# A hybrid attention block on one Trainium2 core: all tensors behind the small constants move back by 64 bytes in their partition

## What is computed

```python
def modulate(x, g, shift, scale):
    return rms_norm(x, g) * (1.0 + scale[:, None, :]) + shift[:, None, :]

# per layer l (latent stream xl, context stream xc)
pl = jnp.split(modulate(xl, g_mix[l], sh1, sc1) @ w_in[l], IN_OFFSETS, axis=-1)
pc = jnp.split(modulate(xc, g_mix[l], csh1, csc1) @ w_in[l], IN_OFFSETS, axis=-1)
oa_l = neighbourhood_attention(qa_l, ka_l, va_l, ka_c, va_c, na_rpb[l])     # 4 heads, "NA"
ob_l = mlstm_output(hb_l, pl[6], ml_head_gain[l])                           # 4 heads, both directions, "ML"
oc_l = blocked_attention(qc_l, concat(kc_l, kc_c), concat(vc_l, vc_c), MLA_SCALE)  # 8 heads, "MLA"
mix_l = jnp.concatenate([flat_heads(oa_l), ob_l, flat_heads(oc_l)], axis=-1) @ w_out[l]
xl = xl + gt1[:, None, :] * mix_l
xl = xl + gt2[:, None, :] * swiglu(modulate(xl, g_ffn[l], sh2, sc2), w_ffn_in[l], w_ffn_out[l])
# the context stream goes through the same weights in layer 0 only
```

## Time and profile before

| what | value |
|---|---|
| median of 3 runs | 2232.1 us |
| lowest and highest run | 2230.06 and 2235.55 us |
| span of the profiled execution | 2231.9 us |
| mean granted TensorE clock in it | 0.979 |
| PE busy | 2102.4 us, 94% of the span |
| DVE, ACT, POOL busy | 53%, 34%, 29% |

### The profile page before, as it was taken

How to read it: one execution, slowest core, us unless ns; L and a number is a source line. 1 busy time by engine, 2 the same in 40 slices (tenths; PEclk the granted TensorE clock), 3 DMA queues, 4 the chain that set the end, 5 groups by cost and what they waited for, 6 DMA issues and landing times.

```text
span 2231.9 us, 30181 instructions
## 1 busy us (share of the span) xinstructions
PE 2102.4 (94%) x11834; PEld 1733.9 (78%) x11834; DVE 1185.5 (53%) x2119; ACT 751.4 (34%) x1221; POOL 644.4 (29%) x820
## 2 busy tenths in 40 slices
PE   7888999989989999999999998889998989999999
PEld 4777788866668888888888877778866657888887
DVE  7467524468875666166436566663368864212111
ACT  4333323456663211111111233423266643222222
POOL 1210301220002333333333430141221014555555
PEclk9999989999999999999999999999899999999999
DMA  7301431110002233233223210021110002322233
GB/s 289 104 19 31 145 102 67 39 47 10 10 10 67 91 127 104 76 114 132 95 95 114 95 50 20 20 68 33 43 48 19 10 10 77 102 95 95 95 95 104
DMA packets 76242, 165.58 MB, mean 74 GB/s; under 512 B 5192, under 2 KB 46664, under 8 KB 75088
## 3 DMA queue, kind: packets, MB, share of 16 engines
q1 hardware_dynamic: 75728, 163.28, 22.0%
q10 hardware_dynamic: 384, 0.47, 0.1%
HBM read 161.63 MB, written 2.10 MB: 73 GB/s over the span
## 4 chain that ended last, share of the span: by engine, by line
PE 79%; DVE 11%; issue 4%; ACT 4%; PEld 1%; POOL 1%; DMA 1%; PEldq 0%; DVEq 0%; SPq 0%; ACTq 0%; POOLq 0%
PE psum L1093 22%; PE psum L1095 21%; PE psum L1094 21%; PE psum L1691 1%; DVE naptlo L2097 1%; PE psum L1144 1%; PE psum L1721 1%; PE psum L1175 1%; PE psum L1446 1%; PE psum L1331 1%; PE psum L1460 1%; PE psum L1397 1%; DVE maplo L2348 1%; PE psum L1216 1%; PE psum L1398 1%
## 5 line engine op out<-in xcount | busy, mean ns | idle before, releaser
L535 POOL TENSOR_TENSOR wlo<-raw,whi 128x256 fp32r<-128x256 f32 x816 | 644.1, 821 | 1579.6 <-ACT whi L560 1579.6
L1093 PE MATMUL psum<-hhi,whi 128*128 128x512 f32 (+1 forms) x1640 | 588.7, 359 | 16.8 <-DVEq L1894 8.6
L1094 PE MATMUL psum<-hlo,whi 128*128 128x512 f32 (+1 forms) x1640 | 579.5, 353 | 0.0
L1095 PE MATMUL psum<-hhi,wlo 128*128 128x512 f32 (+1 forms) x1640 | 578.6, 353 | 0.0
L560 ACT ACTIVATE whi<-raw 128x1024 fp32r<-128x1024 f32 x204 | 215.7, 1059 | 888.2 <-PE psum L1095 881.4
L1093 PEld LDWEIGHTS psum<-hhi,whi 128*128 128x128 f32 x1640 | 313.4, 191 | 72.9 <-issue 18.8
L1095 PEld LDWEIGHTS psum<-hhi,wlo 128*128 128x128 f32 x1640 | 313.0, 191 | 42.5
L1094 PEld LDWEIGHTS psum<-hlo,whi 128*128 128x128 f32 x1640 | 313.3, 191 | 39.9 <-issue 0.2
L2524 DVE TENSOR_TENSOR ffuf<-ffsa,psum 128x768 f32<-128x768 f32 (+1 forms) x44 | 36.1, 821 | 331.5 <-ACT ffsa L1043 324.8
L2509 DVE SCALAR_TENSOR_TENSOR ffmacc<-wm,csil,ffmacc 128x256 f32<-128x256 f32 x336 | 188.7, 603 | 10.1 <-DVE ffmacc L2509 4.9
L1093 PE MATMUL psum<-uhi,whi 128*128 128x512 f32 (+1 forms) x528 | 189.0, 358 | 2.6 <-DVE ulo L2528 1.5
(11 more groups left out here) (329 smaller groups left out, 3385.1 us busy)
## 6 DMA issues: line engine op xcount, KB each, us to landing
raw<-w_stream SPq DMA_DIRECT2D x204, 512.0 KB, 3.7
wm<-w_mod SPq DMA_DIRECT2D x80, 512.0 KB, 4.0
wm<-w_mod SPq DMA_DIRECT2D x8, 1024.0 KB, 13.1
xres<-x_t SPq DMA_DIRECT2D x8, 384.0 KB, 6.3
out<-xres SPq DMA_DIRECT2D x8, 256.0 KB, 2.0
consts<-c_f SPq DMA_DIRECT2D x1, 353.0 KB, 3.6
narpb<-rpb ACTq DMA_DIRECT2D x2, 120.0 KB
mlmask<-c_gate ACTq DMA_DIRECT2D x2, 108.0 KB
```

The costliest lines, as they stand in the source:

```text
L535: nc.gpsimd.tensor_tensor(wlo[:, q % 2, c:c + UW // 4], raw[:, q % RAW, c:c + UW // 4], whi[:, q % 2, c:c + UW // 4], ALU.subtract).then_i ...
L1093: mm(dst, ah, bh, start=first, stop=False)
L1094: mm(dst, ah, bl, start=False, stop=False)
L1095: return mm(dst, al, bh, start=False, stop=last)
```

## The change

`cin` loses its own place and becomes a view of the 64 bytes `amix[:, 1, 0]`, which are written for their own use only in layer 0's FFN, long after `cin` was read. So every tensor declared behind it starts 64 bytes earlier. Three tiles of 64 bytes that nothing uses (`nagap`, `mlgap`, `magap`) are put in: what lies behind them keeps its address. The end of the last tile moves from byte 229312 to 229248.

```diff
-        cin = sb("cin", [P, KT, 2])
+        cin = amix[:, 1, 0]
...
-                     dg=a("nadg", [P, 2, P]), of=a("naof", [P, 256]), s2=a("nas2", [P, 2, 512]),
+                     dg=a("nadg", [P, 2, P]), of=a("naof", [P, 256]), gap=a("nagap", [P, 16]), s2=a("nas2", [P, 2, 512]),
...
-                     den=a("mlden", [P, 2, TT]), ssq=a("mlssq", [P, TT]))
+                     den=a("mlden", [P, 2, TT]), ssq=a("mlssq", [P, TT]), gap=a("mlgap", [P, 16]))
...
-                     r=a("mar", [P, 2, TOK]), mx=a("mamax", [P, 16]), rt=a("mart", [P, SEQ]))
+                     r=a("mar", [P, 2, TOK]), mx=a("mamax", [P, 16]), gap=a("magap", [P, 16]), rt=a("mart", [P, SEQ]))
```

## The result

The kernel after takes 2235.9 us, median of 22 runs (2232.73 to 2242.30), beside 2231.5 us for 22 runs of the kernel before (2225.09 to 2237.86). The ratio of the runs is 1.0023, 95% interval 1.0015 to 1.0032, and the medians are 4.4 us apart: more, where 4.8 us less had been forecast. The number is within the range given and within the 0.3% that I called no change, but its sign is wrong, and the interval excludes the forecast.

The account below looks back on a forecast made before the run. PE was taken as the bound, 79% of the chain, through the cost of one matmul. Terms -2.5 - 0.2 - 0.5 - 0.3 - 1.5 + 0.2 = -4.8 us gave 2227.3 us from 2232.1, range 2218 to 2237 us.

Parts of the forecast that it names:

- (B): Rival: remainder 0 is better than 128, 220 ns a matmul, 11.2 us beyond the forecast: 2216 us; chance 0.12.
- FFN output, layer 1, groups of 8 and of 6: 512-column matmuls on `uhi`, `ulo` fall from 233.3 to 226.7 ns: -2.5 us; group of 6, bound by POOL, -0.2.
- FFN output, layer 0: Blocks pairing 512- and 256-column matmuls: two groups of 8 gain, group of 6 nothing: -0.5 us, bounds +0.3 and -1.0.
- NA's output: NA's output projection: 48 matmuls in layer 1 save 5.4 ns each, -0.3 us; layer 0 nothing.
- MLA: Both layers: 592 moved 512-column matmuls save about 3.3 ns each, three quarters reaching the end: -1.5 us, bounds 0 and -5.8.
- NA attention: `napthi` moves in 104 x 3 matmuls of 256 columns, the width that lost: +0.2 us, bounds -0.3 and +1.0.
- DVE, ACT, POOL, DMA: Work on these engines and the loads keep their durations: 0; DMA bounds 0 and -0.5 us.
- (A): Rival: the start address is not the cause and nothing changes, 2232.1 us; chance 0.15.
- (C): Rival: remainder 0 is worse, 239.9 ns per 512-column matmul, +11.2 us: 2243 us; chance 0.08.
- (D): Rival: 512-column gain in long blocks only, 256-column loss everywhere: -2.5 layer 1, +0.3 layer 0, +1.0 NA: 2231 us; chance 0.10.
- The clock: Granted clock, 0.97 in layer 1's MLA: 0.01 more or less over 206 us is 2 us; moving half-clock stretches could falsify the forecast.

Follow-up runs that it names:

- experiment 1: Kernel of matmuls alone, without the network, varying start of moving tile, start of weights and width; 226.7 to 234.2 ns a matmul at 512 columns.
- `u_only_128`: Kernel before plus one 64-byte gap tile behind `ffmacc`, so `uhi`, `ulo` start at remainder 128; 2226.27 us, ratio 0.9976; again 2226.72 us, 0.9981.
- experiment 5: Second kernel of matmuls alone: two pairs of starts in turn (228.3 to 231.7 ns at 512 columns), and blocks behind one-column matmuls with weights at 0, 64, 128, 192.

## Why the prediction was right or wrong

**The step that failed** is the one that took "remainder 128 by 256" for "a multiple of 128". The rows showed one fast class, `hhi` and `mlo`, and all of it at 128 (`maphi`, at 128 too, stood among neighbours of 234 ns); the change moved tiles to 0, and I wrote myself, under (B), that there was no row for that. I still priced every moved tile by the class at 128. What set the fast ones apart was that `whi` and `wlo` lie at 128 too: experiment 1 gave 226.7 ns at difference 0 for weights at 0, 64, 128 and 192 alike, and 232.4 for a moving tile at 0 with weights at 128. No block of the FFN in the trace of before could separate these two, since every weight tile there lies at 128; but then the two readings deserved like chances, and the reading by difference was not among the rivals at all.

*FFN output, layer 1, groups of 8 and of 6 (-2.5 and -0.2)*: 0 and 0 measured. The price was right: with `uhi` at 128 they are -2.56 and -0.34.

*FFN output, layer 0 (-0.5)*: +1.3. Here the prediction had seen the warning, that 256-column matmuls give back what 512-column ones gain; experiment 1 gives its size (113.3 or 117.8 ns at difference 192, 118.7 at 128, 120.0 at 0), and the blocks themselves went from 117.8 and 113.6 to 119.0 ns. The change got the loss without the gain.

*Left out*: `ffmacc`. It appears in the earlier trace rows between the blocks, and I used it only to subtract a restart. Its start moved too, and costs +0.8 to +0.95 us through blocks whose own tiles stood still.

*NA's output (-0.3)*: -0.06 (12.68 to 12.62 us, with the step to the next instruction); -0.27 where the difference is 0. *MLA (-1.5)*: about -0.2 by the distances at full clock, query projections 233.1 to 232.7 ns and key projections 233.3 to 231.8; nothing of it can be told from the clock. Here the sum counted matmuls that the change could not touch by the difference: the 288 scores and 64 column maxima, 352 of the 592, have their weights in tiles that moved along, `makhi` and `maqhi`. They stayed at 233.2 and 232.9 ns (233.3 and 232.8 after). *NA attention (+0.2)*: about +0.3, from 118.3 to 119.2 ns, although `napthi` and its weights `navhi` moved together; only `naptlo` changed its difference, from 192 to 0. *DVE, ACT, POOL, DMA (0)*: 0; right.

**The rivals.** (A), nothing changes, had the right reading for the largest blocks and for the wrong reason: layer 1's FFN kept 233.3 ns. The Trainium skill, "SBUF — State Buffer", Specifications (TRN2), with its 16-byte lines, would let all starts of experiment 1 cost the same; the measured 226.7, 228.9, 232.1 and 233.3 ns at starts that all begin such a line disagree, and the measurement decides. (B) and (C) fall: no stream settled at 220 or 240 ns; remainder 0 is no class of its own. But the end that (C) stands for, slower, is where the kernel went, in part by a mechanism that I had at +0.3 for layer 0 in (D), the 256-column loss, and in part by `ffmacc`, which no case had. (A), 2232 us, was the nearest in time and (D), 2231 us, the nearest in mechanism, and (D) still kept layer 1's -2.5. That the time fell inside the stated range was luck: the range had been drawn around a gain.

**The clock** was named as what could make the prediction wrong, at 2 us in one stage. It is worth more: the fastest and the slowest run of `u_only_128` are 15.7 us apart, at mean clocks of 0.984 and 0.975.

## What to carry to other kernels

Where long runs of float32r matmuls of 512 columns reload their weights each time, place the moving tile so that its start and the weights' start leave the same remainder by 256: 226.7 instead of 233.3 ns, 3%, for one gap tile, and 3.6 us of this kernel's 2232 by the blocks of `u_only_128`. Do not do it by rule for 256 columns, where that was the slowest place, nor for streams that mix several tiles; measure the mix first. Count only the matmuls whose two operands move against each other, and look at the small matmuls between blocks, whose weights decide how the next block starts. When a trace shows a fast class, ask which property its members share with their partners before naming one of their own, and test it for a few microseconds of chip time with blocks of matmuls alone.

## What the runs showed of the hardware that was not expected

In uniform streams the distance of starts depends on the relative place of two operands in SBUF, not on either alone: by 256, 226.7 ns at difference 0, 228.9 at 64, 232.4 at 128, 233.3 at 192 (experiment 1). Streams settle: after a pause or a group of small matmuls up to ten run at 224 to 236 ns before they reach 226.7, and a group of one-column matmuls with weights at 64 or 192 skips this (experiment 5). At 256 columns a stream at difference 192 has two steady speeds, 113.3 (113.6 in the kernel) and 117.8 ns, and which one it takes can change from one block to the next: moving `ffmacc` alone exchanged the two, from 33.76 and 33.37 us to 33.38 and 33.76.
